# A hybrid decoder step on one core: page units of eight pages against parts of four

## The reference

```
hn = rmsnorm(x); q, k, v, u = split(hn @ w_in)
attn = diff_attend(rope(q), k, v)      # softmax(c=0) - lam * softmax(c=1), 4 heads
s5   = s5_mix(u)                       # diagonal complex state, 32 groups of 16 channels
x = x + concat(attn, s5) @ w_out
x = x + hier_moe(rmsnorm(x))           # top 1 of 4 groups, top 2 of 8 experts in it
y = rmsnorm(x)
```

## Time and profile before

| what | value |
|---|---|
| median of 3 runs | 1534.61 us (1524.88 to 1543.16) |
| the profiled execution | 1536.95 us, span 1535.2 us |
| PE busy in the span | 1303.9 us (85%) |
| DVE, ACT, POOL busy | 522.4, 247.8, 212.3 us |
| mean granted clock of PE | 0.921 |
| moved by DMA | 458.05 MB, mean 298 GB/s |

### The profile page before, as it was taken

One profiled execution on the slowest core, in us unless ns is written; L12 is line 12 of the kernel. 1 busy time (PEld: TensorE's weight loads), 2 busy tenths in 40 slices (PEclk: granted clock), 3 DMA queues, 4 the chain that ended last, 5 costly groups with the idle time before them and its releaser, 6 DMA issues.

```text
span 1535.2 us, 22176 instructions
## 1 busy us (share of the span) xinstructions
PE 1303.9 (85%) x6904; PEld 634.6 (41%) x6904; DVE 522.4 (34%) x1430; ACT 247.8 (16%) x473; POOL 212.3 (14%) x327
## 2 busy tenths in 40 slices
PE   4899898999878877899868999996789999999930
PEld 2344454544424334455443444443344444444410
DVE  1452334442475254555531111125221121111227
ACT  2200111121113122322321000000011111111112
POOL 1102104041301100000010000000112222222111
PEclk9899999999898898999998989986799999999975
DMA  9489979898888886898896979888979999999754
GB/s 351 170 314 307 313 270 301 302 267 287 261 275 283 323 293 207 310 320 317 293 338 267 314 241 325 298 302 273 338 268 346 370 369 365 368 363 370 287 182 190
DMA packets 186433, 458.05 MB, mean 298 GB/s; under 512 B 24177, under 2 KB 24561, under 8 KB 177778
## 3 DMA queue, kind: packets, MB, share of 16 engines
q1 hardware_dynamic: 165906, 394.41, 72.8%
q0 software_dynamic: 20448, 62.59, 12.4%
HBM read 421.92 MB, written 33.80 MB: 297 GB/s over the span
## 4 chain that ended last, share of the span: by engine, by line
PE 67%; DMA 11%; DVE 8%; SPq 6%; issue 4%; DVEq 2%; ACT 1%; POOL 0%; ACTq 0%; PEldq 0%; POOLq 0%
PE WA L1753 48%; PE SC L1753 10%; PE OD L1753 4%; DMA ring<-in_cacheK 4%; DMA ring<-in_cacheV 4%; SPq L481 4%; PE WA L2094 2%; DMA qpad<-h_scratch,idc 1%; SPq L470 1%; DVE st L1097 1%; DVE arena L1722 1%; PE WA L1854 1%; DMA xm<-in_xT 1%; DVE arena L1735 1%; DVE arena L1113 1%
## 5 line engine op out<-in xcount | busy, mean ns | idle before, releaser
L1753 PE MATMUL WA<-arena 128*128 128x512 f32 (+10 forms) x1440 | 354.8, 432 | 23.7 <-issue 13.4
L1753 PE MATMUL WA<-arena,xm 128*128 128x512 f32 (+2 forms) x768 | 313.9, 612 | 9.1 <-DMA arena<-in_w_out 7.0
L1753 PEld LDWEIGHTS WA<-arena 128*128 128x128 f32 (+2 forms) x1440 | 194.3, 197 | 163.7 <-issue 144.7
L1753 PEld LDWEIGHTS WA<-arena,xm 128*128 128x128 f32 (+1 forms) x768 | 122.9, 180 | 166.3 <-issue 156.9
L1753 PE MATMUL SC<-ring,sall 128*32 128x512 f32 x1024 | 141.6, 679 | 45.5 <-DMA ring<-in_cacheV 27.4
L1753 PE MATMUL WA<-xm,arena 128*128 128x512 f32 x192 | 88.8, 611 | 1.7 <-ACT arena L928 1.3
L545 POOL TENSOR_TENSOR st<-st,consts 128x1 f32<-128x1 f32 (+2 forms) x18 | 13.7, 763 | 506.5 <-DVEq L1131 311.5
L1753 PEld LDWEIGHTS SC<-ring,sall 128*32 128x32 f32 x1024 | 29.3, 119 | 128.7 <-issue 77.2
L1753 PE MATMUL OD<-ring,qpad 128*32 128x256 f32 x1024 | 68.1, 411 | 14.7 <-DMA ring<-in_cacheK 14.7
L796 ACT ACTIVATE arena<-WA,st 128x128 f32<-128x128 f32 (+7 forms) x64 | 47.4, 740 | 150.3 <-DVEq L1101 150.3
L1753 PE MATMUL SC<-ring,qpad 128*32 128x256 f32 x1024 | 65.3, 398 | 6.8 <-DMA ring<-in_cacheK 6.8
(11 more groups left out here) (351 smaller groups left out, 1233.2 us busy)
## 6 DMA issues: line engine op xcount, KB each, us to landing
ring<-in_cacheK SPq DMA_DIRECT2D x512, 256.0 KB, 4.5
ring<-in_cacheV SPq DMA_DIRECT2D x512, 256.0 KB, 4.6
arena<-in_w_gu SPq DMA_DIRECT2D x16, 2048.0 KB, 8.2
arena<-in_w_dn SPq DMA_DIRECT2D x16, 1024.0 KB, 11.9
ring<-in_w_gu SPq DMA_DIRECT2D x8, 2048.0 KB, 8.2
xm<-in_w_gu SPq DMA_DIRECT2D x8, 2048.0 KB, 8.2
arena<-in_w_in SPq DMA_DIRECT2D x32, 256.0 KB, 9.5
ring<-in_w_dn SPq DMA_DIRECT2D x8, 1024.0 KB, 11.9
```

Of the source, the lines that this page charges most:

```text
L1753: return pe.matmul(out, lhsT, rhs, start=first, stop=last, **kw)
```

## The change

A unit of eight pages falls into two parts of four (`QP`, `PARTS`): the pages 0, 2, 4, 6 are part 0 and 1, 3, 5, 7 are part 1. The planner's lists hold the parts as units of their own, with half of the cost (0.98 for 1.95), and `PAGE_US` and `PACE` are halved, so that the planned pace of pages stays. SyncE waits before each four pages, in the order of the parts; there are four landing semaphores in place of two, and TensorE waits for and releases each part. A K part has 16 matmuls of 128 columns in place of 256; a V part has four of the eight matmuls, one in each column group. The first part of a sequence's V comes in the plan before `ov` of the one before, the other parts after it. To have the semaphores, `f_g`, used at the end of the kernel, shares eight with `s_xk`.

```diff
-PAGE_US, PAGE_LAG, PACE = 6.0, 3.6, 7.1
+PAGE_US, PAGE_LAG, PACE = 3, 3.6, 3.55
+QP = 4
+PARTS = GRP // QP
...
-                    dec.append((("K", x, t, g, y), 1.95, [(("ov", SPP * x - 1), 0.8)] if x else []))
+                    dec += [(("K", x, t, g, y, p), 0.98, [(("ov", SPP * x - 1), 0.8)] if x else []) for p in range(PARTS)]
...
-                    dec.append((("V", x, y, t, g), 1.95, late))
+                    dec.append((("V", x, y, t, g, 0), 0.98, late))
                     if t + g == 0 and y:
                         dec[-1], dec[-2] = dec[-2], dec[-1]
-            dec.append((("ov", b), 0.4, [(("V", x, y, TURNS - 1, 1), 1.5)]))
+                    dec += [(("V", x, y, t, g, p), 0.98, []) for p in range(1, PARTS)]
+            dec.append((("ov", b), 0.4, [(("V", x, y, TURNS - 1, 1, PARTS - 1), 1.5)]))
...
-    land, gone, due = [0.0, 0.0], [], 0.0
+    land, gone, due = [0.0] * (RING // QP), [], 0.0
...
-            due = max(due + PACE, t - 2 * PACE)
+            due = max(due + PACE, t - 2 * PARTS * PACE)
...
-                sp.wait_ge(s_pgfree, unit + 1)
-                for j, page in enumerate(pages):
-                    sp.dma_start(ring[:, GRP * half + j, :], cache[bass.ds(page, 1), :, :]
-                                 .rearrange("a p n -> p (a n)")).then_inc(s_pg[half], 16)
+                for n, j in enumerate((0, 2, 4, 6, 1, 3, 5, 7)):
+                    if n % QP == 0:
+                        sp.wait_ge(s_pgfree, unit * PARTS + (n // QP + 1))
+                    sp.dma_start(ring[:, GRP * half + j, :], cache[bass.ds(pages[j], 1), :, :]
+                                 .rearrange("a p n -> p (a n)")).then_inc(s_pg[PARTS * half + n // QP], 16)
...
-            def landed(x, unit, half):
-                pe.wait_ge(s_pg[half], 16 * GRP * (SPP * UPB * x + unit // 2 + 1))
+            def landed(x, unit, half, p):
+                pe.wait_ge(s_pg[PARTS * half + p], 16 * QP * (SPP * UPB * x + unit // 2 + 1))
...
-                        last = mm((SC, OD)[g][32 * c:32 * c + 32, 0:256], qpad[:, h, SPP * x + y, :],
-                                  ring[:, GRP * (y % 2) + 2 * c:GRP * (y % 2) + 2 * c + 2, 128 * h:128 * h + 128],
-                                  h + y == 0, h == H - 1 and y == SPP - 1, skip_group_check=True)
-                if y < SPP - 1:
+                        last = mm((SC, OD)[g][32 * c:32 * c + 32, 128 * p:128 * p + 128], qpad[:, h, SPP * x + y, :],
+                                  ring[:, GRP * (y % 2) + 2 * c + p, 128 * h:128 * h + 128],
+                                  h + y + p == 0, h == H - 1 and y == SPP - 1, skip_group_check=True)
+                if y < SPP - 1 or p < PARTS - 1:
                     last.then_inc(s_pgfree, 1)
                     return
...
-                for j in range(GRP):
-
-                    t, q, c = j // 2, j % 2, j % 4
+                for j in range(p, GRP, PARTS):
+
+                    t, q, c = j // 2, j % 2, j // 2
```

More of the change, by code:

```diff
@@ L395, in hymba_step @@
         s_xk = [sem(f"s_xk{k}") for k in range(KD)]
-        s_pg = [sem(f"s_pg{k}") for k in range(RING // GRP)]
+        s_pg = [sem(f"s_pg{k}") for k in range(RING // QP)]
         s_pgfree = sem("s_pgfree")
@@ L431, in hymba_step @@
         s_row, s_col = sem("s_row"), sem("s_col")
-        f_g = [sem(f"f_g{n}") for n in range(NT + 1)]
+        f_g = s_xk + [sem("f_gd")]
         f_gf, f_x, f_sq, f_ms, f_rs, f_out, f_st = (sem(x) for x in (
@@ L501, in _ @@
             weights(slice(0, 1), 0)
-            sp.wait_ge(s_pgfree, RING // GRP + NB * 2 * NPAGE // GRP)
+            sp.wait_ge(s_pgfree, RING // QP + NB * 2 * NPAGE // QP)
             weights(slice(1, 2), 1)
@@ L678, in _ @@
                     todo[unit[0]](*unit[1:])
-            gp.wait_ge(s_pgfree, RING // GRP + NB * 2 * NPAGE // GRP)
+            gp.wait_ge(s_pgfree, RING // QP + NB * 2 * NPAGE // QP)
             gather(0, 1)
@@ L814, in ot, with K @@
                 act.drain().then_inc(s_mix, 1)
-            def K(x, t, g, y):
-                if y < SPP - 1:
+            def K(x, t, g, y, p):
+                if y < SPP - 1 or p < PARTS - 1:
                     return
@@ L1719, in combine @@
                 r = 128 if i < NT else NB
-                dve.wait_ge(f_g[i], 32)
+                dve.wait_ge(f_g[i], 32 + (16 if i < NT else 0))
                 for c in range(2):
@@ L1755, in stats @@
             def stats():
-                pe.nop().then_inc(s_pgfree, RING // GRP)
+                pe.nop().then_inc(s_pgfree, RING // QP)
                 pe.wait_ge(s_cst, 96)
@@ L1873, in ot, with K @@
                 last.then_inc(full_sem("oT", i), 1)
-            def landed(x, unit, half):
-                pe.wait_ge(s_pg[half], 16 * GRP * (SPP * UPB * x + unit // 2 + 1))
-            def K(x, t, g, y):
-                if t == 0 and g == 0 and y == 0:
+            def landed(x, unit, half, p):
+                pe.wait_ge(s_pg[PARTS * half + p], 16 * QP * (SPP * UPB * x + unit // 2 + 1))
+            def K(x, t, g, y, p):
+                if t + g + y + p == 0:
                     pe.wait_ge(s_qbd, 2)
@@ L1883, in K @@
                         pe.wait_ge(s_ad, SPP * x)
-                landed(x, 2 * SPP * t + SPP * g + y, y % 2)
-                if t and y == 0:
+                landed(x, 2 * SPP * t + SPP * g + y, y % 2, p)
+                if t and y + p == 0:
                     pe.wait_ge(s_evac, 2 * (TURNS * x + t) + g - 1)
@@ L1925, in pt, with Vv @@
                 mm(lP, consts[:, C_SUM:C_SUM + 128], mrow[:, 2:3]).then_inc(s_lP, 1)
-            def Vv(x, y, r, g):
-                if r == 0 and g == 0:
+            def Vv(x, y, r, g, p):
+                if r + g + p == 0:
                     if y:
@@ L1932, in Vv @@
                         pe.wait_ge(s_ptw, x + 1)
-                landed(x, SPP * UPB + UPB * y + 2 * r + g, g)
-                for j in range(GRP):
-                    t, q, c = j // 2, j % 2, j % 4
+                landed(x, SPP * UPB + UPB * y + 2 * r + g, g, p)
+                for j in range(p, GRP, PARTS):
+                    t, q, c = j // 2, j % 2, j // 2
                     blk = sall[:, r, 256 * g + 128 * q:256 * g + 128 * q + 128]
                     last = mm(SC[32 * c:32 * c + 32, :], blk[:, 32 * t:32 * t + 32], ring[:, GRP * g + j, :],
-                              r == 0 and g == 0 and j < 4, r == TURNS - 1 and g == 1 and j >= 4 and c > 0,
+                              r + g + p == 0, r == TURNS - 1 and g == 1 and p == PARTS - 1 and c > 0,
                               skip_group_check=True)
                 last.then_inc(s_pgfree, 1)
-                if r == TURNS - 1 and g == 1:
+                if r == TURNS - 1 and g == 1 and p == PARTS - 1:
                     mm(SC[0:32, :], ptn[:, 0:32], dv[:, :], False, True, skip_group_check=True).then_inc(s_pv, 1)
```

## The result

| | median us | runs | profiled execution, us | span | mean clock |
|---|---|---|---|---|---|
| before | 1529.74 (1523.86 to 1543.16) | 4 | 1536.95 | 1535.2 | 0.921 |
| changed | 1552.53 (1550.31 to 1554.37) | 4 | 1550.31 | 1548.5 | 0.926 |

The ratio is 1.0109, with a 95% interval of 1.0067 to 1.0150: slower by about 17 us. The forecast was 1502, and the range ended at 1545. The two medians of this table alone would give 1.015; in the rounds of the experiments the kernel before had medians of 1532.6 to 1538.0 us, and 1552.5 is 0.9 to 1.3% above those.

The account below looks back on a forecast made before the run. TensorE, in program order, was taken to bound the kernel, with 125 us idle in the stages touched, plus lost clock. Page waits -33, copy -6, clock -19, visits +21, narrow K +2 made -35: 1502 us, range 1465 to 1545.

Parts of the forecast that it names:

- the ring's terms: Awaiting and releasing pages by four: shorter page waits, -33 us, their share of clock, and narrower K matmuls, +2 us.
- the order's: The new plan order: shorter waits for the copy, -6 us, their share of clock, and 74 more page visits, +21 us.
- Ring waits, -33: PE's waits for pages in the page stage: earlier slot release takes 30 us off before the tail and 3 in it.
- Copy out of SC, -6: PE's waits for VectorE's copy of decode output, 18.0 us: some go as less prompt work stands between sequences, -6 us.
- Clock, -19: Granted clock in the page stage: 0.5 us gained for each us of PE waits removed, -19 us or so.
- Visits, +21: PE's page stage: 74 more separate visits to page units at 0.28 us each, +21 us.
- narrow K, +2: K matmuls of 128 instead of 256 columns: time goes with columns, so only +2 us for 1024 rounds.
- Weight loads bound the narrow K rounds: Rival at every K part: weight loads lengthen each round to 0.148 or 0.218 us, total 1541 or 1612 us; chance 0.07.
- The DMA engines: Rival at the page ring: DMA engines hold it, page waits fall only 15 us and clock 8, total 1537 us; chance 0.18.
- VectorE is met too early: Rival at six sequence changes: PE arrives 3.6 us sooner and waits for VectorE's copy, +22 us, total 1544 us; chance 0.10.
- three signs of being wrong: Page waits staying over 35 us, K rounds over 0.13 us, or PE's copy waits growing from 18 to over 30 us.

Follow-up runs that it names:

- e1: The changed kernel with the plan of before, each unit's two parts side by side, ring by four: 1517.56 us, ratio 0.9875.
- h1: The kernel before, loading only columns 0 to 255 of every page, the rest of the ring zero, matmuls the same: 1496.42 us, ratio 0.9733.
- e2: The changed plan, but the ring awaited and released by eight pages instead of four: 1635.33 us, ratio 1.0661.
- e5: The changed kernel with V units planned whole again and K parts still planned one by one: 1547.00 us, ratio 1.0057.
- e6: The changed kernel with K units planned whole again and V parts still planned one by one: 1518.71 us, ratio 0.9896.
- e3: The kernel before with each K unit as two groups of 16 matmuls of 128 columns, nothing else: 1540.35 us, ratio 1.0043.
- e13: e1 planned with due times counted by parts, 66 of 651 plan entries standing elsewhere: 1509.36 us, ratio 0.9815.
- e14: The kernel before, ring by eight and wide K matmuls, with e13's plan: 1527.23 us, ratio 0.9942.
- e12: Ring by four with parts side by side as in e1, planned at a pace of 7.3 us for a unit instead of 7.1: 1545.65 us, ratio 1.0072.
- e15: e13 with K units awaited and released whole and their matmuls 256 columns wide: 1514.28 us, ratio 0.9869.
- e10: e6 with the third softmax step of pass 1 moved ahead of a half projection: 1515.74 us, ratio 0.9847.
- e4: The changed kernel with the third quarter's S5 scan moved behind the first pass's page softmax operation on VectorE: 1546.78 us, ratio 1.0079.

## Why the prediction was wrong

The sum was -35; the profiled executions say +14 (to the end of PE's work), and 1552.5 us lies above the range. Split with e1, the ring's terms (-33, 16.5 of clock, +2) were -47 and gave -21; the order's (-6, 3 of clock, +21) were +12 and gave +35. Each is off by about 25 us.

1. **Ring waits, -33.** The cycle of a slot was read rightly: page waits fell by 28.7 us, and they are 20.2 us where I said 15 to 20. The step that failed is the next one, that they come off the time. PE's queue is in program order and the plan's own chains run beside it, so when a page comes earlier PE stands at the next chain's end. Of the page waits taken away, e1 kept 13 of 22 us as less idle time, h1 29 of 39, and the changed kernel none of 28.7. The forecast left 16 us of the waits standing and let nothing come back.
2. **Copy out of SC, -6.** The waits for it fell by 14 us, more than I took. I had written that "the scan must run somewhere and PE may wait for it there", and priced that at nothing. The last quarter's scan left the copy, and the third quarter's came to stand ahead of the page softmax: 8.4 us. All told, page and copy waits fell by 42 us and others rose by as much, since idle time stayed: the page softmax 14.3, attention's chain 15.0, issue 9.6, the rest small ones. I looked at the listing only at the places where a wait stood before, and never at those where the new order could make one. The softmax stood open to be seen there: ("bH", 2) between m2 and m3.
3. **Clock, -19.** Measured -5.8. Its base, 39 us of idle, wasn't there. The rate of 0.5 us for a us of idle is right as an average over a kernel (64.3 for 128.6 in e1, 76.1 for 141.8 before, 90.5 for 198.6 in e2), but the sum used it for a difference, and for differences it doesn't hold: e1 has 13.2 us less idle than before and 11.8 less half clock, h1 28.8 and 11.6, the changed kernel 0 and 5.8.
4. **Visits, +21, and narrow K, +2.** Right. Work is 17 us above the mean of the four plans with parts together (1199.5) for 74 more visits, 0.23 us each (I had 0.28), and 7 and 9 us for e5's 33 and e6's 36. Narrow K is worth 1 (e3), 2.9 (e13 less e14) to 4 us (e1).
5. **The rivals.** "Weight loads bound the narrow K rounds" is out: a part takes 1.01 us from its start to the next piece's, as the columns say. The rule of the Trainium skill (TensorE: Matmul & The Clock Gate, The mechanism) that a weight load hides only behind another row group would have shown as 1.3 us or more; the trace disagrees. The same section also lets a load go ahead into a background weight buffer, and the 1.01 us do not speak against that. The DMA engines don't hold the ring: page waits fell as reckoned. "VectorE is met too early" was right in kind and wrong in place. It was looked for at the copy, where waits fell; it happened at the page softmax and in attention, with 14.3 and 15.0 us. None of the three signs of being wrong came: page waits are 20.2 us, K rounds take 0.11 us, the waits for the copy fell. All three looked at terms of the sum, and the miss was in waits that the sum didn't have. The last V part, forecast to end near 1043 us, ended at 1092.5, and the mean clock from 60 to 1060 us was 0.94.
6. **What I didn't have as a case at all** is that a new plan has other waits of its own. Plans of one kind, at paces of 6.8 to 7.3 us, lie up to 38 us apart (e13 to e12: 19.0 us of idle and 18.7 of clock). A term of 39 us read off one order could not be carried to another; the range was too narrow for that alone. What of the changed order's extra idle time comes of placing parts one by one, and what is this one plan, stays open: the three pairs give 2.3, 1.55 and 0.14%.

## What to carry to other kernels

Where a planner sets the order, price a change in two runs: the mechanism at the old order, then the new order. Here they are -1.25% and +2.3%, and the second hides the first. Count a removed wait at what is left when the next chain's end is reached, not at its length (where the order stayed, 0.6 to 0.75 of it came off the idle time, and with the clock 1.05 to 1.13 us off the end for each us of wait; where the order changed, no idle time did), and look in the new listing at every chain that PE comes to, not only at those that had a wait. And try several plans: the numbers that pace them moved this kernel by 2.6%, and a way of counting that was meant to change nothing may have moved it by 0.6%.

## What the runs showed of the hardware

- Over all kernels here the low level of the granted clock costs 0.46 to 0.61 of PE's idle time (half clock by idle, 60.6 by 132.6 us in e15 and 70.4 by 115.4 in e10), so it follows idle time only roughly. Removing a wait doesn't always buy clock: in e4, 7.4 us less idle came with 5.1 us more at half clock, because the shorter wait that took its place, 2.8 us, was followed by 13.7 us at 0.50, nearly all of them busy; at the wait of 8.4 us 6.8 us were at 0.50, 4 of them still idle.
- Four 32-column groups side by side with 128 columns each: 32 records in 1.01 us, edge included, beside 1.87 us for 256 columns; the loads of 32 columns, reported at 110 ns, stay hidden.

```profile
L1757 PEld LDWEIGHTS SC<-ring,qpad x2048: 106/110/178, 66.9 to 799.8; 128*32 128x32 f32 x187
```

- A visit to a 32-column page part between pieces of prompt work costs PE 0.21 to 0.25 us for the way in and out (7, 9 and 17 us of work for 33, 36 and 74 more visits in e5, e6 and the changed kernel), and it shows in no wait: it is inside the busy time.
